# A decoder block with a mixture of experts on Trainium2: no table of slot numbers, marks that don't wait for the gathers, and an overflow loop that finds its own tokens

## What is computed

```python
def moe(h, router_w, router_b, w1, b1, w2, b2):
    logits = (xt @ router_w + router_b).astype(jnp.float32)
    top_v, top_i = lax.top_k(logits, TOP_K)          # 4 of 32
    gate = jax.nn.softmax(top_v, axis=-1)
    ...
    def expert_block(args):
        xb, e = args
        hc = xb @ w1[e] + b1[e]                      # 1024 -> 2048
        gt = jnp.minimum(hc[:, :D_FF], SWIGLU_LIMIT)
        up = jnp.clip(hc[:, D_FF:], -SWIGLU_LIMIT, SWIGLU_LIMIT)
        glu = gt * jax.nn.sigmoid(SWIGLU_ALPHA * gt)
        return ((up + 1.0) * glu) @ w2[e] + b2[e]    # 1024 -> 1024
    ...
    out = jnp.zeros((T + 1, D), y.dtype).at[buf_tok].add(y)[:T]
```

## Time and profile before

| | us |
|---|---|
| median of 3 runs | 1871.22 (1871.14 to 1871.96) |
| the profiled execution, its own time | 1872.59 |
| its span, first to last instruction | 1870.9 |
| PE busy | 1705.9 (91%) |
| DVE, ACT, POOL busy | 476.8, 271.3, 170.0 |

### The profile page before, as it was taken

One profiled execution on the slowest core, in us unless ns is written; L12 is line 12 of the kernel. 1 busy time (PEld: TensorE's weight loads), 2 busy tenths in 40 slices (PEclk: granted clock), 3 DMA queues, 4 the chain that ended last, 5 costly groups with the idle time before them and its releaser, 6 DMA issues.

```text
span 1870.9 us, 32810 instructions
## 1 busy us (share of the span) xinstructions
PE 1705.9 (91%) x13410; PEld 695.8 (37%) x13410; DVE 476.8 (25%) x995; ACT 271.3 (15%) x550; POOL 170.0 (9%) x324
## 2 busy tenths in 40 slices
PE   5999899888979986899999999999999999999960
PEld 2554444444654452333333333333333333333320
DVE  3012233331233344212212121121211212112116
ACT  3201233232234120000000000000000000000001
POOL 1000000000001004010100101001010010100000
PEclk9988988899989997999999999999999999999985
DMA  7001102004112426999999999999999999999825
GB/s 198 23 23 34 34 11 57 23 1 132 45 48 56 159 79 191 335 381 402 399 390 405 390 402 401 389 401 392 405 397 392 403 388 405 404 390 402 321 102 235
DMA packets 143888, 469.88 MB, mean 251 GB/s; under 512 B 31780, under 2 KB 68796, under 8 KB 110532
## 3 DMA queue, kind: packets, MB, share of 16 engines
q1 hardware_dynamic: 135652, 448.26, 63.4%
q0 software_dynamic: 8192, 21.00, 3.6%
HBM read 456.50 MB, written 16.90 MB: 253 GB/s over the span
## 4 chain that ended last, share of the span: by engine, by line
PE 88%; DVE 5%; ACT 2%; issue 2%; DMA 2%; POOLq 0%; POOL 0%; DVEq 0%; SPq 0%; PEldq 0%; ACTq 0%
PE ps L1480 36%; PE ps L1129 13%; PE ps L1498 12%; PE ps L1502 6%; PE ps L1254 5%; PE ps L1222 3%; PE ps L1423 3%; PE ps L1239 2%; PE ps L1513 1%; PE ps L1454 1%; PE ps L1230 1%; DVE pT L1720 1%; DVE xs L2059 1%; PE ps L1181 1%; DMA ring<-y 1%
## 5 line engine op out<-in xcount | busy, mean ns | idle before, releaser
L1480 PE MATMUL ps<-ring,oT_fox 128*32 128x512 f32 x6144 | 677.2, 595 | 5.7 <-issue 5.5
L1480 PEld LDWEIGHTS ps<-ring,oT_fox 128*32 128x32 f32 x6144 | 186.5, 110 | 474.4 <-issue 471.7
L1498 PE MATMUL ps<-ring,hT 128*32 128x512 f32 x2048 | 264.1, 592 | 0.0
L1977 DVE TENSOR_TENSOR mixT<-ps,mask 128x768 f32<-128x768 f32 x64 | 61.0, 954 | 652.4 <-PE ps L1480 652.4
L1129 PE MATMUL ps<-hT,ring 128*128 128x512 f32 x336 | 151.4, 608 | 13.1 <-ACT hT L891 7.8
L1502 PE MATMUL ps<-ring,hT 128*32 128x256 f32 x2048 | 154.8, 379 | 0.0
L1502 PEld LDWEIGHTS ps<-ring,hT 128*32 128x32 f32 x2048 | 61.3, 110 | 158.4 <-issue 158.4
L1074 ACT ACTIVATE mixT<-mixT 128x768 f32<-128x768 f32 x32 | 27.1, 846 | 621.9 <-DVE mixT L1981 621.9
L1129 PEld LDWEIGHTS ps<-hT,ring 128*128 128x128 f32 x336 | 64.6, 195 | 95.4 <-issue 86.5
L1254 PE MATMUL ps<-hT,ring 128*128 128x512 f32 x176 | 91.7, 669 | 3.1 <-DVE pcT L1763 3.1
L795 POOL COPY pT<-pT 96x32 bf16 (+1 forms) x64 | 13.8, 218 | 838.5 <-ACT hT L1081 838.5
(11 more groups left out here) (282 smaller groups left out, 1261.5 us busy)
## 6 DMA issues: line engine op xcount, KB each, us to landing
ring<-in_expert_w SPq DMA_DIRECT2D x384, 1024.0 KB, 10.1
ring<-in_w_in SPq DMA_DIRECT2D x28, 512.0 KB, 5.1
ring<-y SPq DMA_DIRECT2D x4, 2048.0 KB, 16.8
ring<-in_w_out SPq DMA_DIRECT2D x8, 512.0 KB, 5.9
ring<-in_w_in SPq DMA_DIRECT2D x1, 3168.0 KB, 13.0
xs<-in_x SPq DMA_DIRECT2D x4, 512.0 KB, 5.0
ring<-in_w_in SPq DMA_DIRECT2D x8, 256.0 KB, 3.6
ring<-in_w_proj_nsa SPq DMA_DIRECT2D x16, 128.0 KB, 2.9
```

The lines of the kernel that those rows point to most:

```text
L1480: ins = pe.matmul(wide(ps[TG * j:TG * j + TG, g, :]), xT[b][:, c, TG * g:TG * g + TG], up_slab(c, j), start=(c == 0), stop=(c == NK - 1), ...
L1498: pe.matmul(ps[TG * q:TG * q + TG, 4, :], gT[b][:, 2 * (q // 2) + h, TG * j:TG * j + TG], ring[:, NK + j, at:at + 512], start=False, stop= ...
L1977: return dve.tensor_tensor(to, half, b_up[:, 256 * n:256 * n + 256].unsqueeze(1).broadcast_to([P, NG, 256]), ALU.add)
```

## The change

1. The array `slots` is gone, and with it its tile and fill DMA, the addresses (18 instructions on DVE, counted below), the 16 indirect DMAs on POOL, and two constants made by POOL.
2. DVE no longer waits for the gathers between the marks of the last tile.
3. On PE `turn_x(0, 0, 0)` stands ahead of the eight matmuls for the row numbers (now in a function `spread_rows`). The wait for `rows_ready` has moved ahead of it too.
4. SP waits for the gather of expert 0 alone before it loads the second weights of expert 0.
5. The overflow loop makes its own marks from `placed_at`: more instructions in its body on DVE and PE, fewer on SP. The small operations that list the overflow work on all 128 partitions instead of one.

The 18 instructions are L1927, L1928 and four times L1932 to L1935.

```diff
@@ sync @@
-            sp.wait_ge(consts2, 6)
+            sp.wait_ge(consts2, 5)
...
-            sp.dma_start(slots_d.rearrange("(a b) c -> a (b c)", a=P), fill_sb).then_inc(table_stored, 16)
...
-            for b in range(2):
-                sp.wait_ge(xg_loaded[b], 16)
+            sp.wait_ge(xg_loaded[0], 16)
             for c in range(NK, 12):
                 load_slab(0, c)
...
-            sp.wait_ge(slots_stored, 16 * NT * TOPK)
@@ gpsimd @@
-            step.link(pool.memset(fill_sb, float(NOWHERE + 1)))
...
-            pool.iota(slot_val, pattern=[[TOPK * P, NT], [1, TOPK]], base=1, channel_multiplier=TOPK,
-                      allow_small_or_imprecise_dtypes=True).then_inc(consts2, 1)
-            pool.iota(e_base, pattern=[[SLOTS, E]], base=0, channel_multiplier=0,
...
-            for k in range(TOPK):
-                pool.wait_ge(dest_ready, k + 1)
-                for t in range(NT):
-                    pool.indirect_dma_start(out=slots_d, out_offset=bass.IndirectOffsetOnAxis(
-                        ap=dest_i[:, k, t:t + 1], axis=0), in_=slot_val[:, t, k:k + 1], in_offset=None)\
-                        .then_inc(slots_stored, 16)
             pool.wait_ge(idx_ready, 4)
@@ tensor @@
+            def spread_rows(bank_, first, n, rows):
+                for at in range(2):
+                    for q in range(4):
+                        g = q // 2 if at == 0 else 2
+                        ins = pe.matmul(ps[TG * q:TG * q + TG, bank_, first + at * n:first + (at + 1) * n],
+                                        ident[0:CAP, TG * g:TG * g + TG], rows, start=True, stop=True, tile_position=(0, TG * q))
+                return ins
...
-            pe.wait_ge(rows_ready, 2)
-            for at in range(2):
-                for q in range(4):
...
-            ins.then_inc(table_full, 1)
             pe.wait_ge(bias_ready, 4)
...
+            pe.wait_ge(rows_ready, 2)
             turn_x(0, 0, 0)
+            spread_rows(4, 0, E, row_of).then_inc(table_full, 1)
             expert(0, 0, 0, True, False)
...
+                    e = pe.value_load(extra[0:1, bass.ds(o, 1)], min_val=0, max_val=E - 1)
+                    pe.wait_ge(ov_hot, o + 1)
+                    for t in range(NT):
+                        ins = pe.matmul(ps[0:CAP, 4, 0:2], one_hot[:, t, :], value[:, t, bass.ds(e, 1), :].rearrange("p a v -> p (a v)"),
+                                        start=(t == 0), stop=(t == NT - 1))
@@ vector @@
             take_table(0)
-            for b in range(2):
-                dve.wait_ge(xg_loaded[b], 16)
             mark(NT - 1, 1)
             mark(NT - 1, 2)
-            step.link(dve.tensor_copy(count[0:1, :], routed(NT - 1, 2)[0:1, :]))
+            step.link(dve.tensor_copy(count, routed(NT - 1, 2)))
             take_table(1)
...
-                step.link(dve.scalar_tensor_tensor(dest, chosen, UNPLACED, placed_at, ALU.mult, ALU.add))
-                step.link(dve.tensor_tensor(dest, dest, along(e_base), ALU.add))
...
-                for k in range(TOPK):
-                    step.link(dve.scalar_tensor_tensor(hot, rank, float(k + 1), chosen, ALU.is_equal, ALU.mult))
-                    step.link(dve.tensor_tensor(prod, hot, dest, ALU.mult))
-                    step.link(dve.tensor_reduce(dest_k[:, k, :], prod, AX.X, ALU.add))
-                    dve.tensor_copy(dest_i[:, k, :], dest_k[:, k, :]).then_inc(dest_ready, 1)
...
-                wide = [1, NX, E]
+                wide = [P, NX, E]
...
+                    dve.tensor_scalar(ov_at, placed_at[:, :, bass.ds(e, 1)].rearrange("p t a -> p (t a)"),
+                                      ov_s[:, bass.ds(o, 1)], None, ALU.subtract).then_inc(ov_part, 1)
+                    dve.wait_ge(ov_part, 12 * o + 1)
+                    dve.tensor_tensor(one_hot[:, 0:NT, :], slot_no.unsqueeze(1).broadcast_to([P, NT, CAP]),
+                                      ov_at.unsqueeze(2).broadcast_to([P, NT, CAP]), ALU.is_equal).then_inc(ov_hot, 1)
```

More of the change, by code:

```diff
@@ L315, in hybrid_block @@
         rt = [kk[:, g, :].rearrange("p (a t e) -> p a t e", a=4, t=NT) for kk in (kT_sel_all, kT_win_all) for g in range(G)]
-        logit, over, tied, run, chosen_at, expd, rank, dest = (rt[n // 4][:, n % 4] for n in range(8))
+        logit, over, tied, run, chosen_at, expd, rank = (rt[n // 4][:, n % 4] for n in range(7))
         chosen = chosen_at.rearrange("p t e -> p (t e)").bitcast(F16)[:, 0:NT * E].rearrange("p (t e) -> p t e", t=NT)
@@ L322, in hybrid_block @@
         slot_no = rt[3][:, 2].rearrange("p t e -> p (t e)")[:, 0:CAP]
-        r_bias, e_base, one_e = (rt[3][:, 0, n, :] for n in range(3))
+        r_bias, one_e = (rt[3][:, 0, n, :] for n in range(2))
         cum, many, one_row, count = (rt[3][:, 1, n, :] for n in range(4))
@@ L327, in hybrid_block @@
         top8 = small2[:, 0:32].rearrange("p (t m) -> p t m", t=NT)
-        dest_k, gate_k = (small2[:, 32 + 16 * n:48 + 16 * n].rearrange("p (k t) -> p k t", k=TOPK) for n in range(2))
-        dest_i = small2[:, 64:80].bitcast(I32).rearrange("p (k t) -> p k t", k=TOPK)
-        slot_val = small2[:, 80:96].rearrange("p (t k) -> p t k", t=NT)
+        gate_k = small2[:, 48:64].rearrange("p (k t) -> p k t", k=TOPK)
+        ov_at, ov_row = small2[:, 32:32 + NT], small2[0:CAP, 40:41]
         ss2, rs2, tmp3, tmp4, n_over, r_sum = (small2[:, 96 + 4 * n:100 + 4 * n] for n in range(6))
@@ L340, in hybrid_block @@
         row_of, row_pad = v_fox[0:CAP, 0, 0:E], v_fox[:, 0, E:3 * E]
[L341 removed]
         zero_sb = pcT[0:1, :, :].rearrange("p a s -> p (a s)")
[L343 to L344 removed]
+        ov = [mix_f[:, 1024 * n:1024 * n + NX * E].rearrange("p (o e) -> p o e", o=NX) for n in range(2)]
+        ov_o, ov_e, ov_s = (cmp_neg[:, :, :, :].rearrange("p a b c -> p (a b c)")[:, NX * n:NX * n + NX] for n in range(3))
         def halves(v):
@@ L1439, in _ @@
                 fill_table(NT - 1, part)
-            pe.wait_ge(rows_ready, 2)
-            for at in range(2):
-                for q in range(4):
-                    g = q // 2 if at == 0 else 2
-                    ins = pe.matmul(ps[TG * q:TG * q + TG, 4, at * E:(at + 1) * E], ident[0:CAP, TG * g:TG * g + TG], row_of,
-                                    start=True, stop=True, tile_position=(0, TG * q))
-            ins.then_inc(table_full, 1)
             pe.wait_ge(bias_ready, 4)
-            pe.wait_ge(consts2, 9)
+            pe.wait_ge(consts2, 8)
             def turned_x(b):
```

95 lines of the change are left out of this document (46 added, 49 removed).

## The result

| | before | after |
|---|---|---|
| median, us | 1871.41 (1871.14 to 1871.96, 4 runs) | 1847.22 (1845.72 to 1848.0, 4 runs) |
| the profiled execution | 1872.59 | 1846.65 |
| its span | 1870.9 | 1844.9 |

The ratio is 0.9869, with a 95% interval of 0.9852 to 0.9887: 24.2 us faster, where 20.8 were forecast. It is inside the range, 0.4 us from its lower end. In the profiled executions it is 26.0 us of span. Two things stand behind that number which the prediction did not have, and the experiments found both. 3.5 us came at the end, where it had said "unchanged". And the largest term was there on one chip and absent on two others.

A forecast was written before the change was run, and what follows sets the result against it. PE was taken as the bound, holding 88% of the chain that ended last. The way to expert 0 (7.2) and `up` of expert 0 (13.6) sum to 20.8 us: 1871.2 - 20.8 = 1850.4 us, range 1846.8 to 1858.0.

The forecast's parts named there:

- `up` of expert 0: On PE, expert 0's first half, freed of slot-number writes, takes 23.1 us instead of 36.7: 13.6 gained, largest, least certain step.
- rival (a): PE's stall at expert 0 isn't due to the slot-number writes (instruction feed, say) and stays: 1864.0 us; chance 0.09.
- The way to expert 0: Before expert 0, DVE marks without waiting for gathers, so PE turns at 706.85 instead of 714.08 us: 7.2 us gained.
- rival (b): DVE's marks hold up POOL's issue of the gather: 1.6 us less gain, 1852.0 us; chance 0.12.
- the lower bound: Smallest gain before expert 0: 5.6 us, if POOL's gather issue waits until DVE's marks end (703.9 instead of 702.37).
- after 708.4: Gather for expert 0 landing later than 708.4 us, against 706.8 forecast, would prove the step before expert 0 wrong.
- 0.35 us is what DVE can do by the trace: One POOL slot-write issue beside DVE's two-input operation took 1.32 against 0.97 us; read as DVE's whole effect on an issue.
- The small matmuls and the wait for `rows_ready`: Before `up` of expert 0 on PE: 0.45 us of matmuls hidden by DVE's scaling; wait met 1 us before the gather.
- The end is unchanged: At the kernel's end, behind the experts, nothing was forecast to change: no gain there.
- rival (d): The overflow loop's longer body makes skipped turns dearer, on DVE 3877 ns each at worst: 39 us slower, 1910; chance 0.02.
- The rest: DVE's some 5 us saved, SP's earlier slabs and the expert 2 gather some 30 us earlier all gain nothing.
- rival (c): PE's clock falls otherwise against its work around expert 0: -3 us (1847.4) or +1.7; chance 0.06.

The follow-up runs named there:

- experiment 1: Kernel before without its 16 indirect writes of slot numbers, DVE still computing their addresses: 1856.9 us, ratio 0.9921.
- experiment 4: Kernel after with 16 indirect DMAs of 128 4-byte elements put back on POOL, addresses made by POOL at the start: 1862.06 us, ratio 0.9955 against the kernel before.
- experiment 9: Kernel before with its 16 indirect writes widened from 4 to 64 bytes an element, on the third chip: 1857.37 us, ratio 0.9999.
- experiment 5: Kernel before with its 16 slot-number writes moved behind expert 12 on POOL, on the second chip: 1853.42 us, ratio 0.9983.
- experiment 2: Kernel before without DVE's wait for the two gathers ahead of the last tile's marks, slot-number writes kept: 1865.0 us, ratio 0.997.
- experiment 10: Kernel before with its 16 slot-number writes moved behind expert 12 on POOL, on the third chip: 1853.88 us, ratio 0.9984.
- experiment 11: Kernel after with eight tiny POOL operations added near the start, which shift the later POOL code: 1851.6 us.

## Why the prediction was right, and where it wasn't

**`up` of expert 0, 13.6 us forecast.** Measured 14.5 (36.70 to 22.21), of which 0.8 is the clock: 3.1 us of `up` lay at the low level, 709.7 to 712.8, instead of 4.7. Experiments 1 and 4 measure the writes alone at 13.7 and 12.2 us. The step named as the least certain held on that chip. Two parts of its reasoning did not hold on the third chip. The slow packets were taken as the ground of the stall; on the third chip the packets are slow and PE isn't held, so a slow load is not enough for the stall. The number of writes isn't the cause of the slow load either: as many of 64 bytes leave it alone (experiment 9). And that the median and the profile agree rightly kept the profiler out, but it could not show that all chips behave alike. Against the kernel before of the third chip, the gain of the change is 9.5 us, less than half of the forecast. What PE waits for in the gaps is not shown by any row: they are "issue" on PE and on its weight loads. The feed of PE's instructions, which rival (a) named, fell as a cause apart from the writes, but not as the way by which the writes hold PE. One rival of experiment 5 asked for that, and its chip had no stall. The queue that the profile calls "instruction" (q8) has one packet in 714 to 718 us and the next in 746 to 750, some 4 us after the gaps have ended; in experiment 1 they lie in 714 to 718 and 730 to 734. When such a packet was asked for is not in the trace, so this stays open.

**The way to expert 0, 7.2 us forecast.** 6.9 us at the turning (714.08 to 707.17). The number is right by luck, and rival (b) was right: the issue of the gather is held by the marks. It ends 1.03 to 1.04 us after them in all six runs that have the two side by side. The marks and the issue end at 702.60 and 703.63 in the profile above (699.59 + 3.01, 701.85 + 1.78), at 703.56 and 704.59 in experiment 2, at 703.46 and 704.49 in experiment 4. In the profile after, the marks happened to begin 1.2 us earlier, as routing was through earlier, so the issue took 1.78 us and the loss was 0.6. With routing at its usual time it is the 5.6 us of the lower bound. Experiment 2 gave 5.9, and on the third chip the kernel after has this:

```profile
700.80 3.01 DVE L1856 TENSOR_TENSOR qk<-kT_win 128x1152 f16<-128x1152 f32 x2
701.86 2.99 POOL L743 DMA_INDIRECT oT_nsa<-table,v_win  x1 [127.40 <-DMA table<-hT]
...
708.33 1.51 PE L1428 MATMUL ps<-ident,oT_nsa 96*128 96x96 f32 x8 [3.02 <-DMA oT_nsa<-table,v_win]
```

The turning at 708.33 is the landing "after 708.4" to within 0.1 us that the prediction named as what would show this step wrong. The mis-sized step is "0.35 us is what DVE can do by the trace", and with it "the other 15 show no such loss". Neither was laid beside DVE's rows in the timeline of the kernel before, which has them for the first issue and for the longest:

```profile
719.98 0.29 DVE L1933 TENSOR_TENSOR kT_win<-kT_win,kT_sel 128x128 f32<-128x128 f32 x1
720.03 1.13 POOL L803 DMA_INDIRECT slots<-v_win  x1 [14.73 <-DVE v_win L1935]
...
729.90 0.94 DVE L1954 TENSOR_TENSOR mixT<-kT_win,cmp_neg 1x768 f32<-1x768 f32 x1
730.37 1.32 POOL L803 DMA_INDIRECT slots<-v_win  x1 [0.30 <-issue]
730.88 0.94 DVE L1956 TENSOR_TENSOR mixT<-mixT,kT_win 1x768 f32<-1x768 f32 x1
```

The longest issue began within an operation of DVE that ends at 730.84, and ends 0.85 us after it. Against its usual 0.97 all but the first 0.12 us came after DVE's operation, and with the marks it is the same: 1.03 of 1.16 us. The first issue shows it too: it began within an operation of 0.29 us on two inputs, took 1.13 us, and ended 0.89 us after it. With no operation of DVE beside it the first issue takes 0.97 (experiment 10). Experiment 4 has issues of 1.07, 1.00 and 1.55 us, each ending 0.84 us after the operation on two inputs in which it began. Issues that began within a reduction, which has one input, took 0.96 to 0.97 (732.00 and 733.27 us, beside 0.94 us each).

So the row should have been read as "goes on when the operation in flight is through" instead of "0.35 us longer", and would have given the 1.6 us. How far the hold reaches is less clear. The next operation of the same kind, L1956 above, began 0.04 us after the first had ended and did not hold the issue again. The two marks follow each other without a gap, and on the third chip an issue that began in the first was held through both. In experiment 4 an issue at 719.18 us, 0.01 us behind the start of such an operation, was not held.

The Trainium skill, "SBUF — State Buffer", section "Who interferes with whom", says that a DVE instruction with two inputs in SBUF contends with a GpSimd instruction that reads SBUF, and that the order of issue, not the shape of the operation, decides who blocks. The rows above agree with both. Whether its inference about descriptor generation is wrong they don't tell: the issue of an indirect DMA also has row numbers in SBUF as an input (`v_win` in the row), and no row says which part of it was held.

**The small matmuls and the wait for `rows_ready`.** As forecast: 0.44 us at 708.61, between the turning and `up`, which starts 2.56 us after the turning as before (2.59).

**"The end is unchanged".** Wrong by 4 us, on the good side. The step that failed is that it took a loop whose instructions the change leaves alone to keep its time. POOL's loop was in the trace of before (11.9 us, on the path), and the prediction looked at branches only for DVE and PE. There rival (d) had the sign right for DVE: its 20 steps took 10.7 us before and take 14.3 now (1790.8 to 1805.1), and the load of the results hides them. PE's branches stayed at 214 ns, one at 3337. The Trainium skill, "Runtime: NRT & Kernel Launch", section "Instruction fetch mechanics", says that a taken branch to a target outside the two-page window forces a fetch. Whether a loop straddles a page would depend on where it lies, and experiment 11 fits such a dependence, but at 0.19 us a turn (12.2 against 8.4 us), and no row shows a fetch.

**The rest.** DVE's saved 5 us, SP's earlier slabs and the gather for expert 2 show no gain of their own, as forecast: from 762.50 us on everything is 21.8 us earlier, and keeps its length until the last scatter.

**The sum.** The pieces by themselves, on medians: 14.0 (experiment 1), 5.9 (experiment 2) and 3.5 (POOL's loop) are 23.4 of the 24.2 us measured. So the total lies 3.4 us beyond the forecast mainly by the end, and not by the 3 us that rival (c) put on the clock, for which the range had its lower part. By the two profiles of the third chip the way to expert 0 gives 5.7 us, `up` of expert 0 0.9 and POOL's loop 3.4, which is 10.0 where the medians differ by 9.5.

## What to carry to other kernels

A gap that says "issue" and falls together with a burst of tiny indirect writes is worth removing, but its price was not the same everywhere: measure before and after on more than one chip before the gain is booked. Where such writes can't be avoided, try a wider element: on the third chip 64 bytes instead of 4, in rows of 64 bytes, gave the load its rate back. Look at every loop on the path that does nothing. 21 empty turns cost 8 to 12 us here, and one condition around them saved 9. When an instruction was slowed beside another engine's, ask when it ended in relation to that one, not how much longer it took: a held instruction pays all that is left of the other. And read every instance of a group, not its minimum, median and maximum: the second long issue was hidden between them.

## What the runs showed of the hardware that was not expected

- 2048 writes of 4 bytes within 20 us cost PE 13.7 us on one chip; half of them cost 3.9 us. On two others they cost nothing, by the profile on one and by the time on the other.
- On the third chip these writes brought the load from memory down to 201 GB/s, and as many of 64 bytes left it at 364, the same as with none.
- In six runs POOL's issue of a gather ended 1.03 to 1.04 us after DVE's two marks of 128x1152 and 128x1536 elements, however early it had begun (1.78 to 2.99 us for an issue that takes 1.16 alone). Operations of 0.29 us on two inputs do the same on their scale; reductions of 0.94 us don't.
- The 20 steps of a skipped loop on POOL take 8.4 to 8.9 us or 11.9 to 12.2 with the loop's own instructions unchanged. Eight instructions put far ahead of it moved it from the one to the other.
- What nothing touched varies too: DVE's marks behind the gathers began at 708.74 us in one profile of the kernel before and at 705.26 in the other, so 3.5 us had been won or lost ahead of that.
